# First attention in another order of steps: scores of unit i, mix of i-1, turn of i-2, values of i-3

## The reference, cut to what matters

```python
def diff_attend(q, k, v, lam):          # 4 heads
    s = jnp.einsum('bqhcd,bkhcd->bchqk', q, k).astype(jnp.float32) * DIFF_SCALE
    p = jax.nn.softmax(s, axis=-1)
    p = p[:, 0] - lam * p[:, 1]
    return jnp.einsum('bhqk,bkhe->bqhe', p.astype(v.dtype), v)

def mla_attend(q_nope, q_rope, k_nope, k_rope, v):   # 4 heads
    s = (jnp.einsum('bqhd,bkhd->bhqk', q_nope, k_nope)
         + jnp.einsum('bqhr,bkr->bhqk', q_rope, k_rope)).astype(jnp.float32) * MLA_SCALE
    p = jax.nn.softmax(s, axis=-1)
    return jnp.einsum('bhqk,bkhe->bqhe', p.astype(v.dtype), v)
```

## Time and profile before

| | us |
|---|---|
| three runs | 1577.52, 1578.79, 1578.98 |
| profiled execution, its span | 1577.81, 1576.0 |
| TensorE busy | 1467.2 (93%) |
| VectorE busy | 501.6 (32%) |
| ScalarE busy | 305.5 (19%) |
| chain that ended last | PE 73%, DMA 13%, DVE 8%, issue 3% |
| mean granted clock of TensorE | 0.946 |

### The profile page before, as it was taken

The page is one execution under the profiler, slowest core; times in us unless marked ns, Lnnn a source line. Parts: engine busy times, 40 slices in busy tenths (PEclk is TensorE's granted clock), DMA queues, the critical chain, the costliest instruction groups (busy, mean ns, idle before and its releaser), DMA issues.

```text
span 1576.0 us, 17442 instructions
## 1 busy us (share of the span) xinstructions
PE 1467.2 (93%) x6832; PEld 764.6 (49%) x6832; DVE 501.6 (32%) x896; ACT 305.5 (19%) x449; POOL 15.5 (1%) x34
## 2 busy tenths in 40 slices
PE   4997987999999999999999999999999778899998
PEld 2774455433333333333334334333343466699986
DVE  1545434121121211221121221121121545654565
ACT  3413232001001001001001001001011343444451
POOL 1000001000000000000000000000000000000000
PEclk8999897999999999999999999999999786999999
DMA  9208905699999999999999999999999440555540
GB/s 375 106 27 340 392 39 190 286 425 428 429 421 429 427 429 422 422 428 416 425 425 429 426 428 416 425 428 415 426 426 379 145 145 1 180 193 180 186 144 27
DMA packets 62615, 499.57 MB, mean 317 GB/s; under 512 B 6200, under 2 KB 22616, under 8 KB 34896
## 3 DMA queue, kind: packets, MB, share of 16 engines
q1 hardware_dynamic: 59472, 492.85, 76.4%
q0 software_dynamic: 1648, 5.04, 1.0%
q10 hardware_dynamic: 1456, 1.16, 0.2%
HBM read 497.98 MB, written 1.05 MB: 317 GB/s over the span
## 4 chain that ended last, share of the span: by engine, by line
PE 73%; DMA 13%; DVE 8%; issue 3%; ACT 2%; SPq 1%; PEldq 0%; DVEq 0%; ACTq 0%
PE bank L1418 27%; PE bank L566 22%; PE bank L602 14%; DMA ring<-in_w 10%; PE bank L576 4%; DMA ring<-in_w_ada 2%; PE bank L611 2%; PE bank L622 2%; DVE dk L684 1%; DVE mrows L688 1%; DVE dk L678 1%; PE bank L584 1%; DVE w_lo L429 1%; ACT xn L858 0%; ACT w_hi L422 0%
## 5 line engine op out<-in xcount | busy, mean ns | idle before, releaser
L566 PE MATMUL bank<-ring,xn 128*64 128x512 f32 x2048 | 474.0, 621 | 14.9 <-DMA ring<-in_w 13.5
L566 PEld LDWEIGHTS bank<-ring,xn 128*64 128x64 f32 x2048 | 155.9, 143 | 330.2 <-issue 330.2
L602 PE MATMUL bank<-ring,dq 128*64 128x512 f32 x1024 | 226.8, 595 | 0.0
L673 DVE TENSOR_SCALAR mrows<-bank 128x512 f32<-128x512 f32 x32 | 20.6, 686 | 483.6 <-PE bank L566 483.6
L644 ACT ACTIVATE sq<-mrows 128x512 f32<-128x512 f32 x32 | 19.6, 630 | 792.3 <-DVE mrows L673 792.3
L602 PEld LDWEIGHTS bank<-ring,dq 128*64 128x64 f32 x1024 | 70.6, 137 | 142.8 <-issue 140.1
L429 DVE TENSOR_TENSOR w_lo<-ring,w_hi 128x2048 fp32r<-128x2048 f32 (+1 forms) x44 | 94.2, 2146 | 43.1 <-ACT w_hi L422 42.9
L697 DVE TENSOR_TENSOR dk<-bank,bc 128x512 f32<-128x512 f32 x32 | 22.1, 692 | 256.2 <-PE bank L602 256.2
L422 ACT ACTIVATE w_hi<-ring 128x2048 fp32r<-128x2048 f32 (+1 forms) x44 | 78.3, 1791 | 30.5 <-PE bank L1418 30.3
L1418 PE MATMUL bank<-x_hi,w_hi 128*128 128x256 f32 x256 | 73.6, 287 | 1.8 <-DVE h_lo L1298 1.8
L1418 PE MATMUL bank<-h_lo,w_hi 128*128 128x256 f32 x256 | 73.4, 287 | 0.0
(11 more groups left out here) (353 smaller groups left out, 1517.2 us busy)
## 6 DMA issues: line engine op xcount, KB each, us to landing
ring<-in_w SPq DMA_DIRECT2D x192, 2048.0 KB, 15.7
ring<-in_w_ff SPq DMA_DIRECT2D x32, 1024.0 KB, 5.3
ring<-in_w_ada SPq DMA_DIRECT2D x24, 1024.0 KB, 16.4
ring<-in_w_out SPq DMA_DIRECT2D x8, 1024.0 KB, 8.7
ring<-in_w_in SPq DMA_DIRECT2D x8, 992.0 KB, 26.5
ring<-in_w_in SPq DMA_DIRECT2D x8, 640.0 KB, 9.1
ring<-in_w_ple_gate SPq DMA_DIRECT2D x4, 1024.0 KB, 5.0
xc<-in_ctx SPq DMA_DIRECT2D x1, 1024.0 KB, 5.0
```

Of the source, the lines that this page charges most:

```text
L566: m = pe.matmul(banks[bank_no][mine(i), :], gathered[:, k, mine(i)], rows_of(at + i, 2)[:, k % 2, q * 512:(q + 1) * 512], start=k == 0, st ...
L602: m = pe.matmul(banks[OUT_BANKS[c]][mine(i), :], actT[:, k, mine(i)], rows_of(8 + 2 * j + i, 4)[:, r, c * 512:(c + 1) * 512], start=k == 0 ...
L673: dve.tensor_scalar(gs[:, half * 512:half * 512 + 512], banks[GATE_BANKS[half]][:], LIMIT, None, ALU.min)\
```

## The change

A new list of steps, `skewed_order`, takes the place of `attention_order` in the bank map and on ScalarE, VectorE and TensorE of the first attention. It has a fourth kind of step, "mix". VectorE does its mix there; TensorE, ScalarE and the bank map skip it. Turn and values come one step later than before in relation to the scores. The second block's attention keeps `attention_order`. The work hung in at values 3, 9 and 12 stays there. In the diff below the line of the loop stands once for the three engines; of the edits behind it the first is ScalarE, the next two VectorE, the last TensorE.

```diff
+def skewed_order(n_units):
+
+    order = []
+    for i in range(n_units + 3):
+        for what, u in (("score", i), ("mix", i - 1), ("turn", i - 2), ("value", i - 3)):
+            if 0 <= u < n_units:
+                order.append((what, u))
+    return order
+
-for _what, _u in attention_order(len(UNITS)):
+for _what, _u in skewed_order(len(UNITS)):
     if _what == "score":
         FRONT_TILES += [f"s{_u}_{c}" for c in range(2 if UNITS[_u][0] == "d" else 1)]
-    else:
+    elif _what != "mix":
         FRONT_TILES.append(f"{'pT' if _what == 'turn' else 'av'}{_u}")
...
-            for what, u in attention_order(len(UNITS)):
+            for what, u in skewed_order(len(UNITS)):
...
-                elif u == 9:
+                elif what == "value" and u == 9:
...
-                elif what == "turn":
-                    continue
-                else:
+                elif what == "value":
                     b = take(dve, f"av{u}")
...
-                if what == "score":
+                if what == "mix":
 
                     last = f"s{u}_1" if kind == "d" else f"s{u}_0"
                     wait_read(dve, f"s{u}_0")
...
-                else:
+                elif what == "value":
                     wait_read(pe, f"pT{u}")
```

## The result

The changed kernel takes 1566.18 us (median of five, 1562.24 to 1567.91) where the kernel before takes 1577.52 (five, three of them those above, 1572.86 to 1578.98): 11.3 us less, a ratio of 0.9927 with a 95% interval of 0.9909 to 0.9945. A second set of runs, beside the first variants, gave 1564.39 and 1576.39, ratio 0.9924 (0.9907 to 0.9942). The forecast was 1567.2, range 1561.5 to 1573.5, faster with a chance of 0.90.

A forecast was written before the change was run, and what follows sets the result against it. Differential steps were taken as bound by a chain round all engines, later steps by TensorE; 3.45 us before the ada part plus 7.65 behind made 11.1 less, 1567.2 us, range 1561.5 to 1573.5.

The forecast's parts named there:

- A shorter front passes on whole: Ahead of the expert loop: TensorE's progress triggers later loads, so a front shorter by x ends the kernel x earlier.
- The differential steps: Attention units 0 to 7: VectorE's wait of 1.17 us goes, steps take 3.04 us instead of 4.21.
- The start: First attention steps: clock falls and rises at the old times; ada products start at 154.3 instead of 157.76, 3.45 us earlier.
- The ada part: Ada products up to bc: keeps its length, its last weight chunks meeting no busy queue when asked for earlier.
- Behind bc: Attention after the bc products: turn 6 without its 2.05 us stall, 1.85 us wait at values 11, mixT turns at 211.9.
- The sum: Whole attention: 3.45 us gained before the ada part, 7.65 behind it, 11.1 us in all.
- the slower rival: Second half of the attention: clock stays at half, 14 us slower, 1593; chance 0.05.
- The bounds: Clock phases in the attention: no fall at the start gives 1.3 us, warm behind bc another 1.7; a later fall costs 1.7.
- rival (b): Start or behind bc: the clock stays up, 13 to 16 us less, 1563; chance 0.17.

The follow-up runs named there:

- The filler kernel: Changed kernel with copies first, later root, later scaling and router-stage fillers, plus one throwaway product ahead of the bc products: 1557.46 us, ratio 0.9872.
- the last pair: Changed kernel with copies first, later root and scaling, router-stage fillers: 1555.54 us; the same with the mix put back directly behind its maxima: 1562.51 us.

## Why the prediction was right, and where it was not

**A shorter front passes on whole.** Right. From mixT to the gather 49.42 us in both, from the loop to the end 1296.0 in both, and 1294.9 to 1296.3 in eleven of the twelve other rows of the table, with attentions of 74 to 118 us. The exception is the profile with fillers in the router stage, 1290.9. That execution took 1558.97 us, its kernel's five lie between 1555.99 and 1562.14. From the first turns of the second block on (at 1222.92 us) it is 1.7 and 3.1 us shorter than the two profiles of the changed kernel, and 1.6 and 2.6 of these are the clock: the first large products of that block run at the upper level here, and at the lower one for their first 4 to 6 us there. First this profile, then the later one of the changed kernel:

```profile
1228.99 0.40 PE L1426 MATMUL bank<-w_lo,x_hi 128*128 128x512 f32 x1
...
1231.02 0.63 PE L1426 MATMUL bank<-w_lo,x_hi 128*128 128x512 f32 x1
```

For the other 1.7 to 3.4 us, in the expert loop, I found no cause. So kernels are compared by their medians, and stages only ahead of the loop.

**The differential steps.** Forecast 3.04, measured 3.07, with no idle time ahead of the reciprocal. VectorE is the bound, as said: the copies ahead of the exponentials shorten no such step.

**The start.** Forecast 20.6 us from the first scores to ada (154.3 less 133.7), measured 19.91 and 20.80. The clock fell as assumed and rose sooner: in the first profile before values 0 (142.89), in the later one only behind them, within scores 4 (143.48). Between these two the clock is worth 0.9 us. The 1.3 us that the prediction gives to no fall at all were not shown.

**The ada part.** Forecast to keep its length: 15.50 to bc instead of 15.96. TensorE's wait of 0.34 us for the last weight chunk, at 171.73 before, is gone.

**Behind bc.** Forecast from ada: turn 6 at 25.7, a wait of 1.85 us ahead of values 11, mixT at 57.6. Measured 25.3, 1.80, and 59.1 in one profile, 25.2, 1.80 and 57.6 in the other. Turn 6 does not wait in the first and waits 0.93 us in the second; in both it starts as soon as its mix is made. The first has the fall of the clock behind the wait, which I had as a bound of 1.7 us; it took 1.5.

**The sum.** 11.1 us forecast for the attention, 10.3 and 11.0 measured; the rest of the 11.4 us between the first two profiles is 0.8 of the first scores' earlier time and 0.3 between gather and loop, in which the change has no part. By its parts, 3.45 ahead of ada and 7.65 behind were forecast, 4.1 and 6.2 measured in the first profile, 3.3 and 7.7 in the later. In the first profile it is in part luck that the whole comes so near: a shorter start made up for half of the fall of the clock, which was not in the sum. The median moved by 11.3.

**The rule on transposes** (the Trainium skill, "TensorE: Matmul & The Clock Gate", Part 4) stood as the slower rival: by it the full clock doesn't engage for transposes. The changed kernel kept 1.00 with four transposes per step from 177 to 200 us, so where transposes alternate with products the trace does not agree with it. The rival's mechanism exists all the same, from another cause: with the mix delayed alone TensorE idles 2.8 us per step and the clock is 0.51 from 183 to 204 us.

**What was wrong.** The bounds and rival (b) said that a clock that stays up behind bc gives another 1.7 us. The filler kernel shows 0: turn 6 waits for its mix instead. The prediction's own walk could have told: it has mix 6 end at 179.9 and turn 6 start at 180.0, so a faster TensorE ahead of it has nothing to win. In the changed kernel VectorE works without a gap from the first bc copy (169.55) to the end of that mix (178.01).

The other miss is not the prediction's but that of my expectation for its parts, which had the shift of turns worth 8 us by itself. It was 1.4. The prediction had walked ScalarE's queue for the changed kernel (the copy behind the exponentials, with 0.2 us to spare), and there no values of a differential step wait for a copy. For the shift alone I did not walk it again: with the mix in its old place the copy stands behind exponentials, these behind maxima, these behind a mix. With the queue reordered the shift alone brings 11 us, and both 16 (1577.96 less 1561.93).

What stays open is the price of the whole fall of the clock in the start, why the clock stayed up behind bc with the turns shifted and the copies first, why the expert loop of one profile was 1.7 to 3.4 us shorter, and how much of the 7 us between the last pair is the delayed mix.

## What to carry to other kernels

When a loop runs round several engines in order, give each hand-over a step of its own, and then walk every engine's queue once more for cheap operations that stand behind a waiting one: here one copy in the wrong place hid nearly all that the shift of the turns could give. A part of such a change can be worth nothing, or cost 2%, without the other; price the halves by the queue that each leaves, not by the wait that each removes. A low TensorE clock is worth filling only where nothing else is late just behind it, and a filler must end before the wait that it fills does. When two variants are compared by one profile each, look in which stage they differ: 0.9 us ahead of the place that was changed is not its doing.

## What the runs showed of the hardware that was not expected

- The same wait of 1.80 us brought the clock down in one execution (0.50 from 201.0 to 203.9; eight products of 128x128 took 2.08 us) and not in another (1.16 us). In the start of the same two executions it came up before values 0 in one (1.06 us) and behind them in the other (1.91 us).
- A product of 128x512 in fp32 shows as two instructions that overlap; five of them took 4.56 us at full clock, so its price is 0.9 us and not the mean duration of one record.
- A few fillers in idle stretches kept the router stage at 1.00 where it ran at 0.55, and the gather went from 5.8 to 3.8 us. In one profile the same fillers did not hold it: four took 5.39 us instead of 3.70.
